# Two blocks in one kernel: a weight split moved behind VectorE's adds and sums, and RWKV products sorted by tile shape

## The reference, cut to what matters

```python
h = rms_norm(x, mix_norm_g)
x = x + hybrid_mixer(h, ...)          # four gated branches, one of them RWKV-7
h = rms_norm(x, ffn_norm_g)
x = x + conv_glu_ffn(h, ...)          # "the gated stage": up, conv, silu(gate) * val, down
x = rms_norm(x, final_norm_g)         # end of the first block
# second block, layer 0
proj = rmsnorm(h, norm_mix[0]) @ w_in[0]
mkv  = rmsnorm(mem, mem_norm[0]) @ w_mem_kv[0]
...
def rwkv7_scan(r, w, k, v, a_vec, b_vec):
    # S_t = S_{t-1} diag(w_t) + (S_{t-1} a_t) b_t^T + v_t k_t^T ; y_t = S_t r_t, per head
```

## Time and profile before

| | us |
|---|---|
| median of 3 runs | 1012.99 |
| lowest, highest | 1009.32, 1015.16 |
| the profiled execution | 1011.81 |
| its span, first to last instruction | 1010.0 |
| PE busy | 985.8 (98%) |
| DVE busy | 695.9 (69%) |
| ACT busy | 537.2 (53%) |
| mean granted clock of PE | 0.995 |
| HBM read | 166.96 MB, 166 GB/s over the span |

### The profile page before, as it was taken

How to read it: one execution, slowest core, us unless ns; L and a number is a source line. 1 busy time by engine, 2 the same in 40 slices (tenths; PEclk the granted TensorE clock), 3 DMA queues, 4 the chain that set the end, 5 groups by cost and what they waited for, 6 DMA issues and landing times.

```text
span 1010.0 us, 20599 instructions
## 1 busy us (share of the span) xinstructions
PE 985.8 (98%) x8640; PEld 955.7 (95%) x8640; DVE 695.9 (69%) x855; ACT 537.2 (53%) x689; POOL 35.5 (4%) x28
## 2 busy tenths in 40 slices
PE   6998999999999999998999999999999999999998
PEld 5998898998999999998999999999999899999998
DVE  5678754655788988899886755556777867555553
ACT  5465645445565545466655444443676765435432
POOL 0035050000000000000000000000000000000000
PEclk9999999999999999999999999999999999999999
DMA  7643433332745555545333555555543135565551
GB/s 275 214 169 117 164 98 117 122 127 86 277 168 192 185 208 199 176 167 209 126 126 126 209 192 202 188 182 192 209 145 140 51 126 201 179 207 204 168 206 42
DMA packets 24833, 168.97 MB, mean 167 GB/s; under 512 B 2752, under 2 KB 3264, under 8 KB 4800
## 3 DMA queue, kind: packets, MB, share of 16 engines
q1 hardware_dynamic: 24192, 165.82, 46.9%
q10 hardware_dynamic: 576, 2.20, 0.6%
HBM read 166.96 MB, written 1.05 MB: 166 GB/s over the span
## 4 chain that ended last, share of the span: by engine, by line
PE 80%; DVE 13%; ACT 4%; issue 2%; DMA 0%; DVEq 0%; ACTq 0%
PE G L594 14%; PE G L595 13%; PE G L596 13%; PE D L594 8%; PE D L595 8%; PE D L596 8%; DVE wlo L1792 5%; PE M L595 2%; PE M L594 2%; PE M L596 2%; ACT whi L1275 2%; PE M L811 1%; PE D L1134 1%; PE D L1203 1%; PE M L641 1%
## 5 line engine op out<-in xcount | busy, mean ns | idle before, releaser
L1792 DVE TENSOR_TENSOR wlo<-raw,whi 128x2048 fp32r<-128x2048 f32 x155 | 354.2, 2290 | 125.7 <-ACT whi L1275 125.5
L594 PE MATMUL G<-xh,whi 128*128 128x256 f32 x1280 | 362.7, 283 | 4.4 <-DVE xl L1813 2.9
L595 PE MATMUL G<-xl,whi 128*128 128x256 f32 x1280 | 356.0, 278 | 0.0
L596 PE MATMUL G<-xh,wlo 128*128 128x256 f32 x1280 | 355.9, 278 | 0.0
L1275 ACT ACTIVATE whi<-raw 128x2048 fp32r<-128x2048 f32 x155 | 295.5, 1909 | 57.6 <-PE D L596 47.5
L594 PEld LDWEIGHTS G<-xh,whi 128*128 128x128 f32 x1280 | 241.8, 189 | 12.4 <-DVE wlo L1792 7.0
L595 PEld LDWEIGHTS G<-xl,whi 128*128 128x128 f32 x1280 | 241.6, 189 | 1.3 <-issue 1.2
L596 PEld LDWEIGHTS G<-xh,wlo 128*128 128x128 f32 x1280 | 241.5, 189 | 0.0
L594 PE MATMUL D<-hh,whi 128*128 128x256 f32 x672 | 185.8, 276 | 0.6 <-issue 0.6
L595 PE MATMUL D<-hl,whi 128*128 128x256 f32 x672 | 185.6, 276 | 0.0
L596 PE MATMUL D<-hh,wlo 128*128 128x256 f32 x672 | 185.6, 276 | 0.0
(11 more groups left out here) (398 smaller groups left out, 1383.5 us busy)
## 6 DMA issues: line engine op xcount, KB each, us to landing
raw<-wall_dram SPq DMA_DIRECT2D x155, 1024.0 KB, 4.9
x<-x_dram SPq DMA_DIRECT2D x4, 256.0 KB, 5.4
mem<-mem_dram ACTq DMA_DIRECT2D x1, 1024.0 KB, 4.8
out_dram<-x SPq DMA_DIRECT2D x4, 256.0 KB, 2.2
poolw<-pool_w_dram ACTq DMA_DIRECT2D x1, 768.0 KB, 6.3
cst<-cst_dram SPq DMA_DIRECT2D x1, 448.0 KB, 12.6
lora<-lora_dram SPq DMA_DIRECT2D x1, 256.0 KB, 11.9
sgw<-sg_w_dram SPq DMA_DIRECT2D x1, 256.0 KB, 12.7
```

The source lines that it names most:

```text
L594: mm(out, w_h, hi, start=start, stop=False, skip_group_check=skip)
L595: mm(out, w_h, lo, start=False, stop=False, skip_group_check=skip)
L596: return mm(out, w_l, hi, start=False, stop=stop, skip_group_check=skip)
L1792: signal(tt(wlo[:, pan.slot, 0:w], raw[:, pan.slot, 0:w], f32(whi[:, pan.slot, 0:w]), SUB), "w_lo")
```

## The change

Three edits.

- The third of the splits in front of the adds moves. VectorE's tail call in the gated stage splits one panel less (only where `nu == 2`, that is in this stage), and the step behind the sums splits that panel (`ahead_lo` for `mkv0`-1). ACT's `ahead_hi` keeps ACT's order as it was.
- The split of panel `in0q`, which was behind the sums, goes into `final_norm`, behind the scaling of the second pair of tiles and ahead of the first `xl`.
- `rw_rhs` issues its four 128 x 128 products first and then the four 64 x 128 products; `rw_out` issues products of one shape together with the two halves taking turns, and all 64 x 64 ones at the end. A bank's `start` is set only on the first write into it, and the group check is off. The products are the same.

```diff
-    W += [("ahead", mkv), ("begin", mkv), ("root", 2), ("final_norm",), ("panel", mkv), ("parts", 3)]
+    W += [("ahead_lo", mkv - 1), ("ahead_hi", mkv), ("begin", mkv), ("root", 2), ("final_norm",), ("panel", mkv), ("parts", 3)]
...
+            outs = [M[h % 2][:, 0, (h // 2) * 64:(h // 2 + 1) * 64] for h in range(4)]
             for h in range(4):
+                ins = mm(outs[h], gm[:, 4 * ch + h, 2, :], vn[:, ch, h * 64:(h + 1) * 64],
+                         start=h < 2, stop=ch == 0, skip_group_check=True)
+            for h in range(4 if ch else 0):
                 j, o = h // 2, 64 * (h % 2)
-                out = M[h % 2][:, 0, j * 64:(j + 1) * 64]
-                ins = mm(out, gm[:, 4 * ch + h, 2, :], vn[:, ch, h * 64:(h + 1) * 64],
-                         start=True, stop=ch == 0)
-                if ch:
-                    ins = mm(out, ar[o:o + 64, 2 * j + ch, 0, :], st[o:o + 64, j, :],
-                             start=False, stop=True)
+                ins = mm(outs[h], ar[o:o + 64, 2 * j + ch, 0, :], st[o:o + 64, j, :],
+                         start=False, stop=True, skip_group_check=True)
...
-            for h in range(4):
-                j, o = h // 2, 64 * (h % 2)
+            for j in range(2):
                 for ch in range(2):
-                    out = DB[2][o:o + 64, j, ch * P:(ch + 1) * P]
-                    mm(out, uu[:, ch, h, :], gm[:, 4 * ch + h, 1, :], start=True, stop=False)
-                    ins = mm(out, vn[:, ch, h * 64:(h + 1) * 64], gm[:, 4 * ch + h, 3, :], start=False, stop=ch == 0)
-                    if ch:
-                        ins = mm(out, st[o:o + 64, j, :], ar[o:o + 64, 2 * j + ch, 1, :], start=False, stop=True)
+                    for o in (0, 64):
+                        h = 2 * j + o // 64
+                        mm(DB[2][o:o + 64, j, ch * P:(ch + 1) * P], uu[:, ch, h, :], gm[:, 4 * ch + h, 1, :],
+                           start=j == 0 and ch == 0, stop=False, skip_group_check=True)
+                    for o in (0, 64):
+                        h = 2 * j + o // 64
+                        mm(DB[2][o:o + 64, j, ch * P:(ch + 1) * P], vn[:, ch, h * 64:(h + 1) * 64], gm[:, 4 * ch + h, 3, :],
+                           start=False, stop=ch == 0, skip_group_check=True)
+            for j in range(2):
+                for o in (0, 64):
+                    ins = mm(DB[2][o:o + 64, j, P:2 * P], st[o:o + 64, j, :], ar[o:o + 64, 2 * j + 1, 1, :],
+                             start=False, stop=True, skip_group_check=True)
...
         def final_norm():
             for i in range(4):
                 scaled(x, x, rstd, "fin_g", i, "x_ready", 0)
+                if i == 1:
+                    split_to(PAN["mkv0"] + 3)
                 if i:
                     part(3, i - 1)
...
                 if tail:
-                    more(pan, 1 + nu)
+                    more(pan, nu if nu == 2 else 1 + nu)
```

## The result

| | before | changed |
|---|---|---|
| median, us | 1011.63 | 1003.47 |
| lowest, highest | 1008.57, 1018.49 | 1000.91, 1010.29 |
| runs | 20 | 20 |
| the profiled execution, its span | 1011.81, 1010.0 | 1010.29, 1008.5 |

The ratio is 0.9921, with a 95% interval from 0.9902 to 0.9939: faster by 8 us. But the spans of the two profiles lie only 1.5 us apart, since the profiled execution of the changed kernel was its slowest of 20. Why, is the second half of this document; the first reads the two places of the change.

A forecast was written before the change was run, and what follows sets the result against it. PE, busy 98% of the span, was taken to bound the kernel. Gains of 0.85, 3.0 and 3.3 us sum to 7.15, from a median of 1012.99 to 1005.8 us; range 1001.8 to 1010.0.

The forecast's parts named there:

- Part 1: rw_rhs(1): sorting its eight products by shape takes 1.94 us instead of 2.80, a gain of 0.85.
- Part 2: rw_out: sorted products with alternating halves take 2.6 us instead of 5.58, a gain of 3.0.
- Part 3: Gated end: with two splits ahead, adds and line 632 come 2.2 us earlier; PE's idle falls from 3.70 to 1.5.
- Part 4: Line 632: the clock holds at 1.00, saving 0.9 us there; VectorE starts line 1801 2.95 us earlier.
- Part 5: Moved split of in0q: PE doesn't wait for it, and the memory's scores come 3.3 us earlier.
- Rival 2: RWKV products: halves don't overlap when accumulating, rw_out gains only 0.5 us; whole gain 4.3, time 1008.7; chance 0.12.
- rival 4: RWKV products: weight loads stand open, rw_out takes 10.3 us; whole 2.6 us slower, 1015.6; chance 0.04.
- rival 1: Gated end: the clock falls anyway, gain there 2.2 us, whole 6.05, time 1006.9; chance 0.14.

The follow-up runs named there:

- halves_apart: Changed kernel, but rw_out finishes the lower half of the columns before the upper, sorted by shape inside each; rw_out took 3.85 us.
- rwkv_only: Kernel before with only the sorted RWKV products (rw_rhs and rw_out); median of 12 was 1009.20 us, ratio to before 0.9976.
- in0q_stays: Changed kernel, but in0q's split stays directly behind the sums; 1011.84 us in its one execution, scores 1.66 us earlier than before.

## Why the prediction was right

The changed time and the kind of gain came out as forecast, and nearly every step can be checked:

| term | predicted, us | measured, us |
|---|---|---|
| Part 1, rw_rhs(1) | 0.85 (0.5 to 1.1) | 1.28 |
| Part 2, rw_out | 3.0 (0.5 to 3.2) | 3.03 |
| Part 3, line 632 earlier; idle before it | 2.2; 1.5 | 2.21; 1.50 |
| Part 4, `rtmp` earlier | 2.95 | 2.90 |
| Part 5, the scores earlier by the gated end | 3.3 | 3.24 |
| sum | 7.15 | 7.55 |

**Part 1** was mis-sized: the gain is past its upper bound. The sum had "0.25 for the first change (twice that difference, to be careful)" and again 0.25 at the end, where its own rows gave 0.12 for a change. Line 876 with the first change took 0.93 us, where I had 0.94 and 0.25; line 880 with the change to the panel took 0.59, where I had 0.5 and 0.25. Care put on top of a measured difference made the estimate worse.

**Part 2** had the right size by the right row: line 953's 0.064 a record foretold 2.06 us for 32 records, and they took 1.90. The account of the gain was right in its direction: the overlap is the larger part. Its shares were off. Without any overlap I had 5.05 us and a gain of 0.5; by the estimate above it is 4.64 and 0.87. I had priced 40 records at 0.12 where they take 0.109. Rival 2 would then have cost 2.2 us and not 2.5. What I did not see is that sorting by itself lets halves overlap: `halves_apart` still gains 1.66. The eight 64 x 64 records took 0.07 each with the change behind them, and not line 811's 0.036; there the 0.25 for a change made up for it.

The Trainium skill's rule, in TensorE: Matmul & The Clock Gate, Part 3, that a weight load overlaps only with matmuls of another row group, would have made `rw_out` slower (rival 4). The two halves of the 128 x 64 products use all rows, and their loads of 137 ns are hidden at a distance of 0.055 us from record to record. The trace disagrees with it for this case.

**Parts 3 and 4** held. Line 632 took 1.10 instead of 1.92 with the clock at 1.00. That the clock would hold I had put on one row, the 1.4 us at 169.4. The same trace has the fall at 94 us, behind idle times of 1.28 and 1.07, which I had not looked at; so the reason given was too thin, and that it came out so was in part luck. What a fall of the clock would have cost (rival 1) was not separated from the order of the splits: in `rwkv_only`, where it fell later, `rtmp` came 0.4 us earlier than before and the scores no earlier (34.32 against 34.33).

**Part 5** held in its sum, and `in0q_stays` shows why it was needed. What I had left out is the load of `in0q`: I counted from ACT's copy, which began two microseconds before it was wanted, and ACT's copy, now asked for earlier, stood 1.00 us waiting for the load. It had 3.8 us in hand (470.5 to 474.32), and cost 0.15 only through ACT's root behind it. I had asked which loads would start later, and not which would be wanted earlier.

The scores came at 491.15, 8.44 earlier, where I wrote 7.1. Of that 7.55 are the terms, and most of the rest, 0.77, lies ahead of the first of them (`rw_rhs` at 213.85, not 214.62). The change touches nothing there; over the traces of all kernels this start lies between 212.2 and 214.6, and the three at 214.4 to 214.6 are the three in which the clock fell at 94 us, before among them.

The chance was given without knowing the two paces. Their 5 to 6 us a stage are nearly as large as the gain, and twenty runs of each kernel show it clearly where three might not: 7 of the 20 of the changed kernel lie above 1005, so the median of three may well be one of those.

## What to carry to other kernels

Sort small products by tile shape, and let the column halves take turns within a shape: each change of shape cost 0.14 us (0.09 on the product ahead, 0.05 on the one behind), and across one nothing overlapped. When a wait on another engine is shortened by moving that engine's work, follow the moved work to the next place where it is wanted; here half of the gain came only with the second move, which filled a wait of VectorE with the moved work. And before a difference of half a per cent is read from two profiles, count the matmuls in equal stretches of both: one execution may be at another pace throughout.

## What the runs showed that I had not expected

- Two paces, 0.113 and 0.118 us per 128 x 256 matmul, at a granted clock of 1.00 and a busy share of 100%. Each is held for some 150 us. In 31 of 31 stages the pace behind the second 512-column product was the other than ahead of it, and it also turned at idle times of PE of 0.2 to 0.4 us.
- Products of the same shape in the two column halves run together even where they are issued two products apart (from 227.40 in `halves_apart`, and its 64 x 64 ones).
- The granted clock fell to 0.50 behind idle times of 2.97 and 3.70 us and not behind 1.50 at one place, but at others behind 1.28 and 1.07, and behind 0.63. Nor did it fall at once: in `rwkv_only` the four matmuls of line 632 still ran at 1.00 for 1.1 us.
- One chip runs this kernel at 1012 us and another at 1022, and the ratio of the changed kernel to it was 0.9921 and 0.9951 (0.9917 to 0.9986). The traces from the second chip are not slower at like paces: with both FFNs slow the part behind the scores took 523.5 us there and 523.0 on the first. So the chips may differ only in how often the slow pace comes; no trace of the kernel before from the second chip is there to show it.
